# Routed experts of a decoder layer: rows beyond an expert's first 128 in float32 units of 32

## The chip, the cores and the metric

The kernel runs on one core of one Trainium2 chip, in one launch. The metric is the device time in microseconds. Its median over 3 runs is 2264.56 us (2258.63 to 2267.71) for the kernel before.

## The reference, cut to what matters

One layer of a decoder: a mixer with an output projection, then a mixture of experts, then a gated embedding. 2048 prompt rows and 8 sample rows of 1024 numbers go through it, all in float32. The change is in the experts:

```python
g_sel = argmax(softmax(x @ rg_w + rg_b))                 # one group of 4
top_v, top_i = top_k(e_logits[g_sel], 2)                 # two experts of its 8
expert_idx = g_sel * 8 + top_i                           # two of 32 experts for each row
y[rows of e] = (silu(x @ w1[e]) * (x @ w3[e])) @ w2[e]   # w1, w3: 1024 x 512, w2: 512 x 1024
h = h + weight_0 * y[first choice] + weight_1 * y[second choice]
```

So 4112 rows (two for each of 2056) are shared out over 32 experts. How many each gets follows from the inputs. The router of the reference, worked out on its inputs, gives for experts 0 to 31: 135, 135, 153, 129, 194, 186, 171, 89, 103, 161, 174, 73, 77, 88, 155, 115, 145, 78, 135, 127, 141, 177, 113, 138, 161, 102, 85, 101, 134, 120, 112, 105. 17 experts have more than 128 rows, most of them a few more.

## The kernel before

Phase one is the input projection and the recurrent part, phase two the output projection with norm and router (17 tiles of 128 rows), phase three the experts, and the last phase the gated embedding. In phase three each engine runs its own program, and semaphores tie them; no scheduler moves anything.

**Blocks.** An expert's rows are worked through in blocks of 128 (`block_of`), at least one for each expert. In all that is 49 blocks: 15 experts with one, 17 with two. `blk` holds the first and the end block of each expert, each engine reads them into registers (`span`), and a loop over registers runs the blocks. A weight is split into two float32r parts, `w_hi` (a rounded copy, on ScalarE, `copy` L2149) and `w_lo` (the remainder, on VectorE L2212, for one half of w1 on GpSimd L2070); so are the rows. A product is then three float32r matmuls, hi x hi, hi x lo and lo x hi. On TensorE a block is: 48 matmuls of 512 columns into H1 and H3 (L2113 to L2115), 8 transposes of the next block's rows (L2102) and 4 of `hid` (L2121), and 24 matmuls into the two banks Y (L2132, L2136).

**Weights.** Each of w1, w3, w2 of an expert is 2 MB and comes in two DMAs of 1 MB (`load`, on the SP queue) into one raw buffer for each of the three. A half is fetched again as soon as its split for the expert before is done (`reload`). Four slots of `w_hi` and `w_lo` turn round, so that splits run ahead of the blocks that need them (`parts_ahead`).

**Rows.** GpSimd fetches a list of 128 row numbers (`load_list`), then the rows by an indirect DMA (`gather`), one block ahead. ScalarE copies the result to `y_sb` and sends it to `y_dram`, one block late (`y_out`).

**Start and end of phase three.** Rows of `y_dram` behind the last block are filled at the start of phase three by up to 16 DMAs of 512 KB (L2034). `choices_rows`, on VectorE, works out from which rows of `y_dram` the last phase gathers; it stands behind the last block. The gate weights of the last phase (`in_w_ple_gate`) go through the raw buffers and the same splits as a 33rd expert.

## Time and profile before

| what | value |
|---|---|
| median of 3 runs | 2264.56 us |
| the profiled execution | 2255.27 us, span of its instructions 2253.7 us |
| first matmul of the first block to last matmul of the last | 1061.35 to 1965.96 us |
| TensorE busy over the span | 2149.3 us (95%) |
| VectorE, ScalarE, GpSimd busy | 1430.6 us (63%), 971.0 us (43%), 581.7 us (26%) |
| mean granted TensorE clock | 0.977 of 2.4 GHz |
| moved by DMA | 407.13 MB, 181 GB/s over the span |

Busy time of TensorE counts overlapping matmuls once, from the start of one to its modelled end. What a stream of matmuls costs is the distance from one start to the next. A float32r matmul leaves one pair of records (load of the stationary side, matmul); a plain float32 matmul leaves two such pairs.

### The profile page before, as it was taken

What the parts mean: (1) busy time and instruction counts of PE and PEld (TensorE: products, weight loads), DVE (VectorE), ACT (ScalarE), POOL (GpSimd) and SP (SyncE); (2) the same over time, 40 slices, a digit from 0 to 9 for tenths busy, and PEclk for the clock granted to TensorE, in tenths of its full rate; (3) what the DMA queues carried; (4) which work ended last, traced back from release to release, by engine and by line L of the source; (5) the groups of instructions that cost most, each with busy time, mean ns of one, the idle gap of its engine ahead of it and who ended that gap; (6) DMA issues with size and microseconds to landing.
All of it is one profiled execution on the core that took longest, in us unless ns stands there. A gap on an engine that the chain in (4) does not pass through costs nothing. (4 is left out here: it accounts for less than half of the span.)

```text
span 2253.7 us, 34056 instructions
## 1 busy us (share of the span) xinstructions
PE 2149.3 (95%) x10539; PEld 1773.2 (79%) x10540; DVE 1430.6 (63%) x2866; ACT 971.0 (43%) x1569; POOL 581.7 (26%) x595
## 2 busy tenths in 40 slices
PE   6999999999899999994889999999999999899998
PEld 5878888888788888884778888888888878767775
DVE  5788888888566665564536465665566566846554
ACT  4433344444432222222435465665556465623332
POOL 1121111111244333332121223233332132233332
PEclk9999999999999999996999999999999999999999
DMA  6111110132534333324787677898787778943441
GB/s 231 60 38 66 65 60 37 65 112 92 187 107 136 121 121 117 103 91 147 292 309 256 219 266 289 292 363 289 283 294 260 289 290 305 334 169 125 158 141 49
DMA packets 160333, 407.13 MB, mean 181 GB/s; under 512 B 18835, under 2 KB 22347, under 8 KB 160014
## 3 DMA queue, kind: packets, MB, share of 16 engines
q1 hardware_dynamic: 138518, 337.17, 42.0%
q0 software_dynamic: 14560, 43.11, 5.8%
q10 hardware_dynamic: 7200, 26.22, 2.9%
q8 instruction: 23, 0.38, 0.1%
q14 instruction: 32, 0.26, 0.0%
HBM read 330.12 MB, written 84.82 MB: 184 GB/s over the span
## 5 line engine op out<-in xcount | busy, mean ns | idle before, releaser
L234 PE MATMUL bank<-w_hi,mix_x 128*128 128x512 f32 x816 | 333.3, 408 | 9.9 <-DMA mix_x<-xT_dram 4.0
L236 PE MATMUL bank<-w_hi,mix_x 128*128 128x512 f32 x816 | 323.8, 397 | 0.0
L235 PE MATMUL bank<-w_lo,mix_x 128*128 128x512 f32 x816 | 322.9, 396 | 0.0
L2113 PE MATMUL bank<-w_hi,x_hi 128*128 128x512 f32 x784 | 307.6, 392 | 8.1 <-POOL w_lo L2070 4.6
L2212 DVE TENSOR_TENSOR w_lo<-raw,w_hi 128x2048 fp32r<-128x2048 f32 x130 | 292.6, 2311 | 34.8 <-ACT w_hi L2149 34.7
L2115 PE MATMUL bank<-w_hi,x_lo 128*128 128x512 f32 x784 | 307.1, 392 | 0.0
L2114 PE MATMUL bank<-w_lo,x_hi 128*128 128x512 f32 x784 | 307.1, 392 | 0.0
L2149 ACT ACTIVATE w_hi<-raw 128x2048 fp32r<-128x2048 f32 x130 | 238.8, 1925 | 4.8 <-DMA raw<-in_w 4.8
L2070 POOL TENSOR_TENSOR w_lo<-shared,w_hi 128x2048 fp32r<-128x2048 f32 x31 | 157.2, 5071 | 231.7 <-DMA shared<-hn_dram,entry 131.9
L234 PEld LDWEIGHTS bank<-w_hi,mix_x 128*128 128x128 f32 x816 | 156.7, 192 | 42.0 <-issue 5.1
L236 PEld LDWEIGHTS bank<-w_hi,mix_x 128*128 128x128 f32 x816 | 156.3, 192 | 34.7
L235 PEld LDWEIGHTS bank<-w_lo,mix_x 128*128 128x128 f32 x816 | 156.7, 192 | 29.9
L2113 PEld LDWEIGHTS bank<-w_hi,x_hi 128*128 128x128 f32 x784 | 148.5, 189 | 39.9 <-POOL w_lo L2070 5.0
L2115 PEld LDWEIGHTS bank<-w_hi,x_lo 128*128 128x128 f32 x784 | 148.4, 189 | 31.0
L2114 PEld LDWEIGHTS bank<-w_lo,x_hi 128*128 128x128 f32 x784 | 148.5, 189 | 30.9
L248 POOL TENSOR_SCALAR stat<-stat 128x4 f32<-128x4 f32 (+3 forms) x67 | 13.4, 200 | 514.2 <-ACT junk L716 271.2
L2061 POOL DMA_INDIRECT shared<-hn_dram,entry x49 | 68.2, 1392 | 282.9 <-DMA entry<-list_dram 139.3
L2149 ACT ACTIVATE hidT_hi<-bank 128x128 fp32r<-128x128 f32 x98 | 37.6, 384 | 226.3 <-PE bank L2121 226.3
L2217 DVE SCALAR_TENSOR_TENSOR up<-tanh_h,bank 128x512 f32<-128x512 f32 x49 | 33.5, 684 | 157.4 <-ACT tanh_h L2174 157.4
L2132 PE MATMUL bank<-w_hi,hidT_hi 128*128 128x512 f32 x392 | 126.6, 404 | 0.0
L2132 PE MATMUL bank<-w_lo,hidT_hi 128*128 128x512 f32 x392 | 122.3, 393 | 0.0
L2149 ACT ACTIVATE w_hi<-shared 128x2048 fp32r<-128x2048 f32 x64 | 119.7, 1921 | 4.7 <-DMA shared<-in_w 3.9
(316 smaller groups left out, 4222.1 us busy)
## 6 DMA issues: line engine op xcount, KB each, us to landing
raw<-in_w SPq DMA_DIRECT2D x128, 1024.0 KB, 8.5
shared<-in_w SPq DMA_DIRECT2D x64, 1024.0 KB, 8.6
y_dram<-y_sb ACTq DMA_DIRECT2D x50, 512.0 KB, 6.9
xT_dram<-mix_x SPq DMA_DIRECT2D x34, 512.0 KB, 3.5
mix_x<-xT_dram SPq DMA_DIRECT2D x34, 512.0 KB, 4.5
shared<-in_w_in SPq DMA_DIRECT2D x24, 512.0 KB, 6.5
small<-in_x_prompt SPq DMA_DIRECT2D x16, 512.0 KB
xr_sb<-in_x_prompt SPq DMA_DIRECT2D x16, 512.0 KB
```

The costliest lines, as they stand in the source:

```text
L234: pe.matmul(bank[:, :], x_hi[:, k, :], wh[:, k, :], start=(k == 0), stop=False)
L235: pe.matmul(bank[:, :], x_hi[:, k, :], wl[:, k, :], start=False, stop=False)
L236: ins = pe.matmul(bank[:, :], x_lo[:, k, :], wh[:, k, :], start=False, stop=(k == KD - 1))
L2061: pool.indirect_dma_start(out=rows_in[:, :], out_offset=None, in_=hn_dram[0:NT * P + NS, :], in_offset=bass.IndirectOffsetOnAxis(ap=entry[ ...
L2070: pool.tensor_tensor(w_lo[slot(j, 0)][:, cols], raw[0][:, cols], w_hi[slot(j, 0)][:, cols].bitcast(F32), ALU.subtract).then_inc(w1_lo, 1)
L2113: pe.matmul(bank[:, :], x_hi[:, k, :], wh[:, k, :], start=(k == 0), stop=False)
L2114: pe.matmul(bank[:, :], x_hi[:, k, :], wl[:, k, :], start=False, stop=False)
L2115: ins = pe.matmul(bank[:, :], x_lo[:, k, :], wh[:, k, :], start=False, stop=(k == KD - 1))
L2132: pe.matmul(Y[n][:, :], hidT_hi[:, k, :], col(w, k, n), start=(k == 0 and w is wh), stop=False)
L2149: return act.activation(out, in_, ACT.Copy)
L2212: dve.tensor_tensor(w_lo[slot(j, m)][:, cols], raw[m][:, cols], w_hi[slot(j, m)][:, cols].bitcast(F32), ALU.subtract).then_inc(w1_lo if is ...
L2217: STT(up[:, :], tanh_h[:, :], 1.0, H1[:, :], ALU.add, ALU.mult).then_inc(up_done, 1)
```

## The change

An expert's first 128 rows are computed as before, in one block of three float32r products (`expert` in place of the loop over `block_of`). Its rows beyond 128 are computed in units of 32 (`tail`), at least one for each expert, in plain float32 with the raw weights. With the counts above that makes 40 units: 25 hold rows, and 15 experts have one of unused rows; expert 4 has three, experts 5, 6, 9, 10, 21 and 24 have two.

A unit keeps its 32 rows (transposed, `xT_t`) as the stationary side and streams the weights. Four column tiles of the array each take a quarter of the hidden columns: of w1 and w3 together 256 columns, 8 times over the depth, so 32 matmuls; then 16 matmuls of 256 columns for w2. Units belong to one expert ahead: while expert e's block is computed, the units of expert e + 1 run, with raw w1, w3 (now in two buffers `raw13` that take turns) and w2; with the last block those of expert 0. In each round of the loop the 12 matmuls of `first_down` (one half of expert e's down projection, 512 columns each) stand between the unit's own steps. They start their bank anew in each round, so they are computed once for each unit.

The weights have three slots in place of four, and splits run at most one matrix ahead. The order on SP, GpSimd, ScalarE and VectorE is written anew around that. `choices_rows` now stands between two splits of the last expert. Unused rows of `y_dram` are filled in phase two, by one DMA of 258 rows from HBM to HBM in each of 16 tiles. The bounds of an expert's units are read into registers within the expert (on TensorE between the two lots of transposes). VectorE has 6 more small instructions of 32 columns where it works out `blk`.

```diff
+TAIL = 32
+TILES = P // TAIL
+MAXT = NE + (SEQ + NS) * 2 // TAIL
+SPARE = (MAXT + 1 - NE) * TAIL // NT
...
+                                if r == P:
+                                    sp_.dma_start(y_dram[bass.ds(u * SPARE + NE * (P + TAIL), SPARE), :], x_rows[0:SPARE, :]).then_inc(spare_filled, 16)
...
+                def behind(e):
+                    return 0 if isinstance(e, int) and e == NE - 1 else e + 1
...
+                        def expert(e, two, j):
+                            wait_lo(sp_, e, 2, 1)
+                            load(behind(e), 1 - j, 2)
+                            sp_.wait_ge(h3_mm, e + 1)
+                            for m in range(2):
+                                if last(e):
+                                    load_gate(m)
+                                else:
+                                    load(e + 2 if not isinstance(e, int) or e < NE - 2 else 0, j, m)
...
+                        def first_down(k):
+                            wh, wl = w_down(w_hi), w_down(w_lo)
+                            pe.matmul(Y[0][:, :], hidT_hi[:, k, :], wh[:, k, 0:512], start=(k == 0), stop=False)
+                            pe.matmul(Y[0][:, :], hidT_hi[:, k, :], wl[:, k, 0:512], start=False, stop=False)
+                            pe.matmul(Y[0][:, :], hidT_lo[:, k, :], wh[:, k, 0:512], start=False, stop=(k == KF - 1))
+
+                        def tail(i, e, two, j):
+                            for m in range(2):
+                                for c in range(2):
+                                    pe.wait_ge(*tail_in(e, two, j, m, c))
+                            pe.wait_ge(t_x_in, i + 1)
+                            w13 = raw13[1 - j][:, :].rearrange("p (m k n) -> p m k n", m=2, k=KD)
+                            for k in range(KD):
+                                for q in range(TILES):
+                                    ins = pe.matmul(UP_T[q * TAIL:(q + 1) * TAIL, :].rearrange("p (m n) -> p m n", m=2), xT_t[:, k, :],
+                                                    w13[:, :, k, q * P:(q + 1) * P], start=(k == 0), stop=(k == KD - 1))
+                            ins.then_inc(t_up_mm, 1)
...
+                            pe.wait_ge(hidT_lo_ready, 2 * e + 2)
+                            first_down(0)
+                            pe.wait_ge(t_rows, 16 * i + 32)
+                            first_down(1)
+                            tail_transposes()
+                            pe.wait_ge(t_hid, i + 1)
+                            pe.transpose(HID_T, hid_t[:, :], ident[:, :]).then_inc(t_hid_tp, 1)
+                            first_down(2)
+                            first_down(3)
...
+                            for k in range(KF):
+                                for q in range(TILES):
+                                    ins = pe.matmul(DOWN_T[q * TAIL:(q + 1) * TAIL, :], hidT_t[:, k * TAIL:(k + 1) * TAIL],
+                                                    w2[:, k, q * width:(q + 1) * width], start=(k == 0), stop=(k == KF - 1))
+                            ins.then_inc(t_down_mm, 1)
...
+                        def tail(i, e):
+                            act.wait_ge(t_up_mm, i + 1)
+                            act.activation(tanh_t[:, :], UP_T[:, 0:P], ACT.Tanh, scale=0.5).then_inc(t_tanh, 1)
+                            tail_x(i + 1)
+                            act.wait_ge(t_hid_tp, i + 1)
+                            copy(hidT_t[:, :], HID_T).then_inc(t_hidT_in, 1)
...
+                        def expert(e, two, j):
+                            split(e, two, j, 1)
+                            if not isinstance(e, int) or e > 0:
+                                y_halves(e - 1)
+                            split(e, two, j, 2)
+                            if not isinstance(e, int) or e > 0:
+                                y_out(e - 1)
+                            first, end = span(act, behind(e))
+                            act.wait_ge(h1_mm, e + 1)
+                            act.activation(tanh_h[:, :], H1[:, :], ACT.Tanh, scale=0.5).then_inc(tanh_done, 1)
+                            split(e + 1, *follow(two, j), 0)
```

TensorE, one block before, from the last up matmul to the end of the block (`bank` is a PSUM bank, `shared` here the gathered rows; in all fences of this part, register rows and rows that only repeat are left out):

```order
L2115 MATMUL bank<-w_hi,x_lo 128x512
L2102 MATMUL bank<-ident,shared 128x128 x4
L2121 MATMUL bank<-ident,hid 128x128
L2102 MATMUL bank<-ident,shared 128x128 x4
L2121 MATMUL bank<-ident,hid 128x128 x3
L2132 MATMUL bank<-w_hi,hidT_hi 128x512 x2
L2132 MATMUL bank<-w_lo,hidT_hi 128x512 x2
L2136 MATMUL bank<-w_hi,hidT_lo 128x512 x8
L1964 COMPARE_AND_BRANCH
```

And now, with the unit in its loop between the transposes and the second half of the down projection (`raw_1` holds raw w1 and w3 of the next expert; a row 32x256 is one column tile's matmul):

```order
L2222 MATMUL bank<-w_hi,x_pair 128x512
L2236 MATMUL bank<-ident,hid 128x128 x3
L2185 MATMUL bank<-raw_1,xT_t 32x256 x32
L2173 MATMUL bank<-w_hi,hidT_hi 128x512
L2167 MATMUL bank<-ident,rows_t 128x32 x8
L2198 MATMUL bank<-ident,up 128x128
L2175 MATMUL bank<-w_hi,hidT_lo 128x512
L2209 MATMUL bank<-shared,hidT_t 32x256 x16
L2238 COMPARE_AND_BRANCH
L2242 MATMUL bank<-w_hi,hidT_hi 128x512
```

48 matmuls of the new shape, 8 transposes of 32 rows and one of 128 came in; of the 24 down matmuls 12 stand inside the loop.

ScalarE, the last block before (both splits of the gate's first half stood ahead of it, the row L2149 on `shared`):

```order
L2149 ACTIVATE w_hi<-shared 128x2048 x2
L2174 ACTIVATE tanh_h<-bank 128x512
L2149 ACTIVATE y_sb<-bank 128x512 x2
L2149 ACTIVATE hidT_hi<-bank 128x128
L2149 ACTIVATE hidT_hi<-bank 128x384
L2149 ACTIVATE x_hi<-bank 128x512 x2
L2149 ACTIVATE w_hi<-raw 128x2048 x2
```

ScalarE, the last expert now (`raw_1` in the first of these rows on it holds the gate's first half):

```order
L2312 ACTIVATE tanh_h<-bank 128x512
L2256 ACTIVATE w_hi<-raw_1 128x2048 x2
L2256 ACTIVATE hidT_hi<-bank 128x128
L2256 ACTIVATE hidT_hi<-bank 128x384
L2276 ACTIVATE tanh_h<-bank 128x128
L2256 ACTIVATE xT_t<-bank 128x256
L2256 ACTIVATE hidT_t<-bank 128x128
L2256 ACTIVATE y_t<-bank 128x256
```

The split of the gate's first half moved from ahead of the last block's tanh to behind it, and stands ahead of the copies of `hidT_hi` there.

VectorE, the last expert now (`shared` in the rows of L2365 to L2371 is scratch room):

```order
L2351 TENSOR_TENSOR w_lo<-raw_1,w_hi 128x2048 x2
L2363 TENSOR_SCALAR rowbase<-lead 128x34
L2365 TENSOR_TENSOR shared<-rowbase,ecap 128x1088
L2371 TENSOR_REDUCE rowbase<-shared 128x34
L2351 TENSOR_TENSOR w_lo<-shared,w_hi 128x2048 x2
L2385 SCALAR_TENSOR_TENSOR up<-tanh_h,bank 128x512
L2394 TENSOR_TENSOR hidT_lo<-bank,hidT_hi 128x384
L2351 TENSOR_TENSOR w_lo<-raw_1,w_hi 128x2048 x2
L2356 SCALAR_TENSOR_TENSOR up<-tanh_h,bank 128x128
```

`choices_rows` (L2363 to L2373) stands ahead of the split of w2 and of `up`, and the split of the gate's first half ahead of the unit's own first step; before, both came outside the last block.

## Rows read from the trace of the kernel before

**Rows 1.** The page: busy time by engine, then the span in 40 slices
```profile
PE 2149.3 (95%) x10539; PEld 1773.2 (79%) x10540; DVE 1430.6 (63%) x2866; ACT 971.0 (43%) x1569; POOL 581.7 (26%) x595
...
PE   6999999999899999994889999999999999899998
...
PEclk9999999999999999996999999999999999999999
```

**Rows 2.** Windows (us, each engine's busy us, PEclk, DMA share, GB/s)
```profile
1153.00:1368.00 215.00, 214.53 (x1008) 176.82 (x1007) 117.93 (x119) 113.59 (x127) 54.65 (x31) 1.00 0.73 262
...
1060.00:1065.00 5.00, 3.65 (x9) 2.88 (x10) 3.28 (x3) 3.32 (x2) 0.00 (x0) 0.50 0.95 361
...
1075.00:1080.00 5.00, 4.53 (x27) 3.97 (x27) 2.83 (x6) 1.75 (x4) 0.58 (x1) 1.00 1.05 400
...
954.00:1008.00 54.00, 54.00 (x285) 45.80 (x283) 31.68 (x105) 14.77 (x40) 19.11 (x23) 1.00 0.25 84
```

**Rows 3.** Timeline of TensorE: blocks' first matmuls (start us, length us), last end
```profile
1061.35 0.79 PE L2113 MATMUL bank<-w_hi,x_hi 128*128 128x512 f32 x1 [3.53 <-DVE x_lo L2204]
...
1152.93 0.39 PE L2113 MATMUL bank<-w_hi,x_hi 128*128 128x512 f32 x1
...
1296.60 0.39 PE L2113 MATMUL bank<-w_hi,x_hi 128*128 128x512 f32 x1
...
1314.50 0.39 PE L2113 MATMUL bank<-w_hi,x_hi 128*128 128x512 f32 x1
...
1964.67 1.29 PE L2136 MATMUL bank<-w_hi,hidT_lo 128*128 128x512 f32 x5
```

**Rows 4.** Groups of the page: shapes xcount, busy us, mean ns, idle before
```profile
L2113 PE MATMUL bank<-w_hi,x_hi 128*128 128x512 f32 x784 | 307.6, 392 | 8.1 <-POOL w_lo L2070 4.6
L2212 DVE TENSOR_TENSOR w_lo<-raw,w_hi 128x2048 fp32r<-128x2048 f32 x130 | 292.6, 2311 | 34.8 <-ACT w_hi L2149 34.7
L2149 ACT ACTIVATE w_hi<-raw 128x2048 fp32r<-128x2048 f32 x130 | 238.8, 1925 | 4.8 <-DMA raw<-in_w 4.8
L2070 POOL TENSOR_TENSOR w_lo<-shared,w_hi 128x2048 fp32r<-128x2048 f32 x31 | 157.2, 5071 | 231.7 <-DMA shared<-hn_dram,entry 131.9
```

**Rows 5.** The chain that ended last: 24 float32r matmuls, 4 float32 (8 records)
```profile
2007.66 5.48 PE bank L2414 x24
2013.14 3.43 PE bank L2399 x8
```

**Rows 6.** Timeline of TensorE: eight transposes; matmuls with 8 output partitions
```profile
1982.51 1.04 PE L2390 MATMUL bank<-ident,hs 128*128 128x128 f32 x8
...
2222.86 0.66 PE L2390 MATMUL bank<-ident,hs 8*128 8x8 f32 x8
...
2228.96 0.39 PE L2414 MATMUL bank<-w_hi,hT_lo 128*128 128x512 f32 x1
2229.28 3.60 PE L2399 MATMUL bank<-shared,hz 128*8 128x512 f32 x8
2232.81 0.50 PE L2414 MATMUL bank<-w_hi,hT_hi 128*128 128x512 f32 x1
2233.14 0.40 PE L2414 MATMUL bank<-w_lo,hT_hi 128*128 128x512 f32 x1
```

**Rows 7.** DMA issues: KB each, median us to landing
```profile
raw<-in_w SPq DMA_DIRECT2D x128, 1024.0 KB, 8.5
...
entry<-list_dram POOLq DMA_DIRECT2D x50, 0.5 KB, 4.7
shared<-hn_dram,entry POOLq DMA_INDIRECT x50, 6.4
```

**Rows 8.** Timelines of the last block: ScalarE, VectorE
```profile
1965.46 1.13 ACT L2149 ACTIVATE y_sb<-bank 128x512 f32<-128x512 f32 x2
...
1962.73 0.17 DVE L2233 TENSOR_SCALAR rowbase<-lead 128x34 f32<-128x34 f32 x1
...
1967.14 4.49 DVE L2212 TENSOR_TENSOR w_lo<-raw,w_hi 128x2048 fp32r<-128x2048 f32 x2
```

**Rows 9.** Timeline of SP in phase two: the load of rows, once in each tile
```profile
850.70 0.33 SPq L1203 DMA_DIRECT2D xr_sb<-in_x_prompt  x1
...
877.47 0.33 SPq L1203 DMA_DIRECT2D xr_sb<-in_x_prompt  x1
```

More of the change, by code:

```diff
@@ L2187, in _ @@
-                        act.sem_inc(y_stored, 16)
+                            if not last(e):
+                                x_halves(e + 1)
+                            with act.Fori(first, end) as i:
+                                tail(i, e)
+                        act.sem_inc(t_stored, 16)
+                        act.sem_inc(t_y_in, 1)
                         x_halves(0)
-                        split(0, 0, 1)
-                        split(0, 0, 2)
-                        all_blocks(act, block_of, after)
+                        each_expert(act, expert)
@@ L2242, in choices_rows @@
                             dve.wait_ge(place_steps, 4)
[L2243 removed]
+                            STT(yrow[:, :, :], rowbase[:, :, :], float(-NE * (CAP - P) - P), place[:, :, :], ALU.add, ALU.add).then_inc(place_steps, 1)
                             dve.wait_ge(place_steps, 5)
[L2246 to L2251 removed]
```

474 lines of the change are left out of this document (270 added, 204 removed).

## The prediction

> **What bounds the kernel now.** I read the page first: TensorE is busy 95% of the span, next VectorE with 63%, and TensorE's busy share is 8 or 9 tenths in nearly every slice [rows 1]. The windows say the same of phase three: of 215 us TensorE is busy 214.53, VectorE 117.93, ScalarE 113.59, at the full clock, with DMA at 0.73 [rows 2]. So a change in phase three is worth what it takes from TensorE's stream plus what it adds in waits. The timeline gives the price of a block: one begins at 1296.60, the next at 1314.50, 17.90 us [rows 3]. The count is 784 / 16 = 49 blocks [rows 4], which the row counts of the 32 experts give too. 49 x 17.90 = 877.1 us of the 904.6 between 1061.35 and 1965.96; the other 27.5 are stalls. The first four blocks take 91.6 us instead of 71.6, 20.0 lost while the weights of three experts come in; the remaining 45 take 813.0 instead of 805.5, 7.5 lost [rows 3].
>
> The prices on TensorE: 24 float32r matmuls of 512 columns in 5.48 us are 0.228 each [rows 5]. Four float32 matmuls of 512 columns (8 records) take 3.43 us [rows 5], so one of 256 columns takes 0.43 us by itself. Eight 128 x 128 transposes start 0.109 us apart (1.04 less the last one's length, over 7), eight of 8 x 8 about 0.065 apart [rows 6]; I take the latter as what one pair of weight load and short matmul costs at the least.
>
> **The change part by part, for TensorE.** The sum is made against the profiled execution, 2255.27 us, 0.4% under the median of 2264.56; I add its result to the median.
>
> Removed: 17 second blocks, 17 x 17.90 = -304.3 us. What is left of a block stays as it was: 48 + 12 + 12 matmuls and 12 transposes.
>
> Added: 40 units. Each has 32 + 16 = 48 float32 matmuls of 256 columns. The trace has no neighbouring matmuls in different column tiles, so their overlap is the unknown price. Bounds: all four tiles at once, 48 x 0.43 / 4 = 5.2 us; none at once, 48 x 0.43 = 20.6 us. With full overlap the 96 pairs also cost 96 x 0.065 = 6.2 us if the pairs are what limits. For the likeliest case I take full overlap, and 5.6 us, between 5.2 and 6.2, since part of the pairs can be issued ahead while longer matmuls run.
> Nine transposes: 8 of 32 rows between 0.065 and 0.109 each, one at 0.109: 0.8 us.
> Changes between wide and narrow outputs: from 2228.96 to 2229.28 lie 0.32 us where 0.23 is the pitch, so going in costs 0.09; coming out, 8 records of 0.429 end at 2232.71, the next matmul starts at 2232.81 and its follower 0.33 later instead of 0.23, 0.2 in all [rows 6]. Twice in and out per unit: 0.6 us.
> Sum of a unit 7.0 us, x 40 = +280. In 8 of the units the 12 matmuls of `first_down` are computed once more: 8 x 12 x 0.228 = +21.8.
> Stream in all: -304.3 + 280 + 21.8 = -2.5 us. The work saved and the work added are nearly equal, because 15 experts pay for a unit of unused rows.
>
> Steps within a unit that could make TensorE wait: from the end of the up matmuls, tanh on ScalarE and two steps on VectorE of 128 columns, some 1.2 us, lie beside two lots of `first_down` (1.4) and the transposes (0.8); the two copies to `hidT_t` and `xT_t` beside the other two lots (1.4). I cost these at nothing; without that cover they cost about 1 us each, +40 to +80 us in all.
>
> **Other engines.** With one unit an expert takes 17.9 + 7.0 = 24.9 us. ScalarE then has six splits of 1.9 [rows 4] and some 5 us of copies, 17 us; VectorE five of 2.3 and some 4.5, 16 us; GpSimd one of 5.1 and the issue of two gathers, whose list and rows land 4.7 and 6.4 us after it [rows 7], a unit or an expert ahead. All under 24.9. The tightest place is w3: ScalarE splits it after the unit's last copy, 2 x 1.9 us, then VectorE 2.3 more, some 7.0 us with the copy; TensorE wants it after 12 down matmuls and 24 up, 8.2 us. It fits with 1.2 us to spare. Cost zero.
>
> DMA: an expert brings 6.3 MB of weights, 0.5 of rows, 0.5 of results, some 0.3 for the unit. At the 400 GB/s that a full DMA share shows [rows 2] that is 19 us of 24.9. w2 of the next expert is asked for about 1.2 us before the end of h3, and wanted by the unit's down matmuls 8 to 9 us after it; 2 MB at 400 GB/s are 5.3 us, plus the 2 to 3 us that a DMA of 1 MB with nothing ahead needs besides (8.5 us to landing, median, mostly for two in flight [rows 7]). It just fits.
>
> Fill of unused rows: 1.06 MB per tile in phase two, where TensorE has no idle time and the DMA share is 0.25 [rows 2]. At 400 GB/s that is 3 to 5 us of DMA per tile of 26.8 us (850.70 to 877.47 [rows 9]), well before the loads of the next mixer rows. Cost 0, at the most 16 x 1 us. In turn the start of phase three is rid of 8 MB.
>
> **Start of phase three.** The first unit needs w1 and w3 of expert 1; w3 and w2 of expert 0 stand ahead of them: 8.4 MB from 1057 on at 400 GB/s, landed at about 1079 to 1081. TensorE would be there at about 1077, after a first block that runs in part at half the clock (PEclk 0.50 up to 1065 [rows 2]). So 4 us of wait and 3 of clock, less what later experts wait: 6 us where 20 were lost, -14. The 7.5 us of later stalls also go, since the weights have 24.9 us for each expert: -7.
>
> **Last expert.** Here two things are new. `choices_rows` takes 4.4 us (1962.73 to 1967.14 [rows 8]) and stands ahead of the split of w2. And ScalarE must split the gate's first half before it copies `hidT_hi`, but SP asks for the gate weights after the end of h3 and behind w2 of expert 0: about 4 MB after that, 13 to 15 us to landing of the second half, then the split of 1.9. TensorE meanwhile has only the unit's up matmuls. `hidT` comes about 18 us after h3 instead of 2, then VectorE splits two halves (4.5 us) before the unit's own steps. The expert ends 31 us after h3 instead of 14: +17. Results are copied behind one more split (3.7 us) where they were copied at once (1965.46 [rows 8]): +3, since the last gathers wait for them.
>
> Sum: -2.5 - 14 - 7 + 17 + 3 = -3.5 us, so 2264.56 - 3.5 = 2261 us. Within full overlap the ends are 6.4 us for a unit (-24 us, -27 in all) and 7.8 (6.2 + 1.0 + 0.6; +32, +28 in all, together with 0.5 us here and there for the loop's branches): 2236 to 2292.
>
> **Rivals.**
> *Overlap of two, not four (36%).* A float32 matmul leaves two pairs of records one behind the other [rows 5]. If TensorE starts matmuls strictly in order and the second pass must wait until the first has left its tile, then only the second pass of one tile and the first of the next run together. A matmul then costs one pass, 0.214 us, up to 0.24 with the start: 48 x 0.214 = 10.3, to 11.5 us. That is +4.7 to +5.9 us a unit, +188 to +236 in all, some 5 less for waits that it hides: 2445 to 2490 us. This is the rival on the other side; it decides as soon as a unit's 48 matmuls take more than about 5.9 us (+0.5%). For it speaks the order in the trace; against it, that nothing in the trace shows a busy tile holding up another.
> The Trainium skill ("TensorE: Matmul & The Clock Gate", Part 3, What overlaps and what doesn't) says that matmuls keep strict program order in start and end, which is the premise of this rival; its Measured speedup section gives 2.38 for three column tiles, one matmul in each, which is the premise of full overlap. By the one the kernel takes some 2465 us, by the other about 2261; no run of before shows either.
> *The units are cheap (27%).* The pairs are no limit and the transposes take 0.065: 6.4 us a unit, 2238 us, 2230 to 2252. For it: TensorE's queue can run ahead while 0.228 us matmuls are in front.
> *No overlap at all (5%).* 48 x 0.43 = 20.6 us: +15 x 40 = +600, 2860 us. Only if float32 excludes tiles side by side.
> *The last expert or the start costs more than I see (in the 32% of the likeliest).* A clock that falls in the wait would add up to 5 us.
>
> **Chances.** Full overlap 59%: of it 27% cheap units (faster), 32% around my number, of which some 3 faster, 20 within 0.5% (2253 to 2276; about what a measurement of this kernel can tell from no change), 9 slower. Overlap of two 36%, none 5%. So faster 0.30, same 0.20, slower 0.50. The likeliest case is full overlap, with its own range 2236 to 2292; since a third of the chance lies at 2445 to 2490, the range for 8 in 10 goes from 2236 to 2490, leaving out the case of no overlap and the thin ends.
>
> **What would show it.** In the changed kernel's timeline: 40 rounds of 48 matmuls in narrow tiles; the 32 of the up part span 3.5 to 4.2 us with full overlap, 6.9 to 7.7 with two, 13.7 with none. Experts with one unit begin 24.9 us apart (29.6 to 30.8; 39.9). The first expert is some 6 us longer, in the last one TensorE idles about 10 us before `first_down`, released by ScalarE's `hidT_hi`, which waited for `in_w_ple_gate`. Idle time of TensorE at w3's `w_lo` or at raw w2 in most experts would show my two margins (1.2 us, and the DMA of w2) wrong. Phase two should keep its 27 us a tile.

## The result and the profile after

The changed kernel takes 2297.53 us (median of 4 runs, 2296.34 to 2298.68) beside 2261.6 for the kernel before on the same chip: ratio 1.0156, 95% interval 1.0129 to 1.0183, slower by 36 us. The profiled execution took 2297.97 us, its span is 2296.4 against 2253.7. The spans differ by 42.7 us where the medians differ by 36, because the profiled execution of before (2255.27 us) is faster than any of the four behind its median; what follows accounts for the 42.7.

The page of after, lines that answer to [rows 1] and [rows 7]: busy time, TensorE by slices, the granted clock, then DMA issues (KB each, median us to landing), the third of them the new fill of unused rows.

```profile
span 2296.4 us, 39441 instructions
PE 2159.8 (94%) x13407; PEld 1680.9 (73%) x13408; DVE 1445.2 (63%) x2830; ACT 966.7 (42%) x1607; POOL 651.5 (28%) x641
PE   6999999999999999994899999999999999789998
PEclk9999999999999999996999999999999999899999
raw<-in_w SPq DMA_DIRECT2D x130, 1024.0 KB, 15.7
mix_x<-xT_dram SPq DMA_DIRECT2D x34, 512.0 KB, 5.3
y_dram<-in_x_prompt SPq DMA_DIRECT2D x16, 1032.0 KB, 8.0
```

The windows of phase three, first after, then before (busy us and count of each engine, clock, DMA share, GB/s; the other end of each window is the end of the last block):

```profile
1085.00:2007.00 922.00, 885.85 (x6984) 631.29 (x6984) 546.17 (x469) 502.70 (x574) 320.25 (x173) 0.98 0.74 273
```

```profile
1061.00:1966.00 905.00, 885.64 (x4116) 728.45 (x4116) 533.28 (x509) 510.08 (x539) 251.29 (x128) 0.99 0.80 291
```

TensorE's busy time in phase three is the same to 0.2 us: 17 blocks went, and 40 units with 8 repeated `first_down` weigh as much. What grew is idle time, 19 to 36 us. The other part of the loss lies ahead of phase three. By the timeline, the first block starts at 1085.16 where it started at 1061.35 [rows 3]. The difference of the spans is therefore 42.7 us = 23.8 before the first block + 17.5 in phase three (922.1 us for 904.6) + 1.4 behind it.

### The profile page after: what moved, and what is told of

It reads as the page before. It is cut to its first block and busy times, and to the rows that moved or that the text cites. A ratio compares the mean times of both kernels' runs of the same rounds, so it can differ in the third digit from the quotient of the medians.

```text
span 2296.4 us, 39441 instructions
## 1 busy us (share of the span) xinstructions
PE 2159.8 (94%) x13407; PEld 1680.9 (73%) x13408; DVE 1445.2 (63%) x2830; ACT 966.7 (42%) x1607; POOL 651.5 (28%) x641
## 5 line engine op out<-in xcount | busy, mean ns | idle before, releaser
L2220 PE MATMUL bank<-w_hi,x_pair 128*128 128x512 f32 x512 | 203.8, 398 | 12.8 <-DVE w_lo L2351 8.7
L2222 PE MATMUL bank<-w_hi,x_pair 128*128 128x512 f32 x512 | 200.6, 392 | 0.0
L2221 PE MATMUL bank<-w_lo,x_pair 128*128 128x512 f32 x512 | 200.6, 392 | 0.0
L2121 POOL TENSOR_TENSOR w_lo<-raw,w_hi 128x2048 fp32r<-128x2048 f32 x31 | 141.8, 4575 | 197.6 <-ACT w_hi L2256 197.5
L2351 DVE TENSOR_TENSOR w_lo<-shared,w_hi 128x2048 fp32r<-128x2048 f32 x66 | 148.4, 2288 | 16.7 <-PEq L1204 10.9
L2185 PE MATMUL bank<-raw,xT_t 128*32 128x256 f32 x2560 | 150.9, 389 | 2.2 <-DMA raw<-in_w 2.2
L2113 POOL DMA_INDIRECT rows_t<-hn_dram,entry_t x40 | 63.8, 1595 | 291.2 <-DMA entry_t<-list_dram 198.3
L2220 PEld LDWEIGHTS bank<-w_hi,x_pair 128*128 128x128 f32 x512 | 96.7, 189 | 44.8 <-DVE w_lo L2351 20.9
L2185 PEld LDWEIGHTS bank<-raw,xT_t 128*32 128x32 f32 x2560 | 81.4, 112 | 60.5 <-issue 12.8
L2559 PE MATMUL bank<-w_hi,hT_hi 128*128 128x512 f32 x272 | 113.9, 419 | 2.0 <-DVE hT_lo L2632 2.0
L871 DVE SCALAR_TENSOR_TENSOR qkT<-qkin,cwt,qkT 128x128 f32<-128x128 f32 x384 | 110.3, 349 | 3.4
L2222 PEld LDWEIGHTS bank<-w_hi,x_pair 128*128 128x128 f32 x512 | 96.7, 189 | 20.7
```

What stands on the lines that cost most here:

```text
L871: st.do(STT(cv[:, k, :], src, cwt[:, k, j:j + 1], cv[:, k, :], ALU.mult, ALU.add))
L2121: pool.tensor_tensor(w_lo[0][:, cols], raw_of(e, j, 0)[:, cols], w_hi[0][:, cols].bitcast(F32), ALU.subtract).then_inc(w1_lo, 1)
L2185: ins = pe.matmul(UP_T[q * TAIL:(q + 1) * TAIL, :].rearrange("p (m n) -> p m n", m=2), xT_t[:, k, :], w13[:, :, k, q * P:(q + 1) * P], sta ...
L2220: pe.matmul(bank[:, :], x_hi[:, k, :], wh[:, k, :], start=(k == 0), stop=False)
L2221: pe.matmul(bank[:, :], x_hi[:, k, :], wl[:, k, :], start=False, stop=False)
L2222: ins = pe.matmul(bank[:, :], x_lo[:, k, :], wh[:, k, :], start=False, stop=(k == KD - 1))
```

## Where the time lies in the trace

**The unit.** TensorE's timeline of after, an expert with one unit:

```profile
1496.68 0.49 PE L2236 MATMUL bank<-ident,hid 128*128 128x128 f32 x3
1497.10 3.66 PE L2185 MATMUL bank<-raw,xT_t 128*32 128x256 f32 x64
1500.69 0.50 PE L2173 MATMUL bank<-w_hi,hidT_hi 128*128 128x512 f32 x1
...
1502.28 0.68 PE L2167 MATMUL bank<-ident,rows_t 32*128 32x32 f32 x8
1503.26 0.33 PE L2198 MATMUL bank<-ident,up 128*128 128x128 f32 x1 [0.30 <-DVE up L2358]
...
1504.91 1.93 PE L2209 MATMUL bank<-shared,hidT_t 128*32 128x256 f32 x32
1506.78 0.50 PE L2242 MATMUL bank<-w_hi,hidT_hi 128*128 128x512 f32 x1
```

Read starts, not lengths: the up part holds TensorE for 1500.69 - 1497.10 = 3.59 us (64 records, two for each float32 matmul), the down part for 1506.78 - 1504.91 = 1.87. Together 5.46 us for 48 matmuls, 0.114 each where I took 0.43 for one by itself. The starts of the single records, which the timeline puts together into one row, show how: in all 40 units they come in fours, the four within some 0.02 us and the next four 0.216 us later at the full clock. Each matmul has two records, so a step of four matmuls takes 2 x 0.216 = 0.43 us, the price that I took for one: the four column tiles overlap in full.

**Phase two.** SP's timeline of after (issue of the load of rows, then the fill, then a sample's state; answers to [rows 9]):

```profile
841.34 0.33 SPq L1209 DMA_DIRECT2D xr_sb<-in_x_prompt  x1
841.71 0.52 SPq L1238 DMA_DIRECT2D y_dram<-in_x_prompt  x1
842.89 0.43 SPq L1276 DMA_DIRECT2D shared<-in_state_C  x1
870.21 0.33 SPq L1209 DMA_DIRECT2D xr_sb<-in_x_prompt  x1
...
901.97 0.33 SPq L1209 DMA_DIRECT2D xr_sb<-in_x_prompt  x1
```

These two tiles take 28.9 and 31.8 us where one took 26.8 [rows 9]; from 902 on, where no state is loaded any more, it is 26.6 again. The fill stands ahead of the state's load on the same queue. The six loads of the state land 7.5 to 13.0 us after their issue where they took 4.8 to 5.6. What VectorE waits for, 600 to 1040 us (us in total, times, longest), before and after:

```profile
DVE shared L1679 <- DMA shared<-in_state_C: 3.6, 6, 0.9
```

```profile
DVE shared L1687 <- DMA shared<-in_state_C: 33.4, 6, 9.0
```

**First and last expert.** TensorE's timeline of after, rows that waited (in brackets us, releaser): the first expert, then the last.

```profile
1105.56 0.47 PE L2236 MATMUL bank<-ident,hid 128*128 128x128 f32 x1 [5.33 <-ACT xT_t L2256]
1109.70 6.11 PE L2185 MATMUL bank<-raw,xT_t 128*32 128x256 f32 x64 [2.17 <-DMA raw<-in_w]
...
1979.34 1.37 PE L2236 MATMUL bank<-ident,hid 128*128 128x128 f32 x4 [3.93 <-DVE hid L2390]
1980.64 5.84 PE L2185 MATMUL bank<-raw,xT_t 128*32 128x256 f32 x64
1994.63 0.77 PE L2173 MATMUL bank<-w_hi,hidT_hi 128*128 128x512 f32 x1 [8.15 <-DVE hidT_lo L2394]
```

The up part, 3.66 us long elsewhere, takes 5.8 to 6.1 behind such waits. Windows of after on the up part of the first expert, of the one shown above, and of the last (columns as for the windows above):

```profile
1109.80:1115.30 5.50, 5.50 (x60) 2.67 (x64) 2.28 (x1) 0.00 (x0) 3.55 (x3) 0.55 1.03 395
1497.20:1500.60 3.40, 3.40 (x64) 1.88 (x64) 2.87 (x2) 1.47 (x3) 3.33 (x1) 1.00 1.03 418
1980.70:1986.00 5.30, 5.30 (x61) 2.59 (x64) 0.00 (x0) 0.00 (x0) 0.00 (x0) 0.58 1.03 415
```

The granted clock was 0.55 and 0.58 of 2.4 GHz behind the idle time, near the lower of its two levels, and 1.00 where TensorE had been busy. The DMA share is full in all three windows, so it does not tell them apart. The up part of the first expert starts 24.5 us behind the first block, when the raw weights of expert 1 have landed. SP's timeline shows one reason why they are late:

```profile
1079.45 0.96 SPq L2058 DMA_DIRECT2D raw<-in_w  x2
1083.99 0.88 SPq L2058 DMA_DIRECT2D shared<-in_w  x2
1084.91 6.61 SPq L2058 DMA_DIRECT2D raw<-in_w  x3
```

The first row is w3 of expert 0. SP then waits for two splits (`lo_ready`, `w1_lo`) before it asks for w2 and for the weights of expert 1, 4.5 us later, at 1083.99. In the last expert, ScalarE and VectorE show what TensorE's 8.15 us wait for:

```profile
1988.73 1.91 ACT L2256 ACTIVATE w_hi<-raw 128x2048 fp32r<-128x2048 f32 x1 [16.85 <-DMA raw<-in_w_ple_gate]
1993.55 0.94 DVE L2394 TENSOR_TENSOR hidT_lo<-bank,hidT_hi 128x128 fp32r<-128x128 f32 x2 [13.80 <-ACT hidT_hi L2256]
```

ScalarE waits 16.85 us for the gate's weights, and its copy of `hidT_hi` stands behind their split. The first expert takes 39.2 us, the last 43.3. In between, 23 experts with one unit take 25.63 us on average (25.65 where the unit is empty, 25.62 where it holds rows), and a further unit 8.81.

## The experiments

| kernel | median us | ratio to before (95%) | first block | phase three | behind it |
|---|---|---|---|---|---|
| before | 2261.6 | | 1061.4 | 904.6 | 287.7 |
| after | 2297.5 | 1.0156 (1.0129 to 1.0183) | 1085.2 | 922.1 | 289.2 |
| b_fill | 2281.0 | 1.0095 (1.0074 to 1.0116) | 1084.1 | 907.4 | 287.8 |
| a_fill_later | 2276.7 | 1.0076 (1.0059 to 1.0092) | 1065.2 | 920.5 | 289.0 |
| a_fill_act | 2284.4 | 1.0103 (1.0085 to 1.0121) | 1073.7 | 921.9 | 289.2 |
| a_last | 2283.9 | 1.0102 (1.0085 to 1.0119) | 1084.9 | 904.5 | 293.8 |
| a_down_by_tile | 2405.6 | 1.0635 (1.0610 to 1.0661) | 1094.5 | 1025.4 | 288.8 |
| a_two_units | 2509.7 | 1.1104 (1.1077 to 1.1132) | 1081.8 | 1131.6 | 288.9 |
| a_early_gate | 2266.0 | 1.0015 (1.0003 to 1.0026) | 1067.2 | 910.0 | 288.9 |
| a_skip | 2240.0 | 0.9902 (0.9884 to 0.9921) | 1067.2 | 885.6 | 292.9 |
| a_skip_all | 2216.3 | 0.9792 (0.9776 to 0.9808) | 1067.7 | 858.0 | 288.8 |
| a_first_x | 2217.6 | 0.9803 (0.9790 to 0.9817) | 1066.3 | 860.8 | 290.2 |

The last three columns are the start of the first block, from there to the end of the last, and the rest of the span, in us of the profiled execution. Each ratio is taken to the kernel before as measured beside that run, 2260.7 to 2262.1 us. Four kernels have the phase two of after (after, a_last, a_down_by_tile, a_two_units), and their first blocks start between 1081.8 and 1094.5: a start of one execution holds to some us, and so does the 23.8.

**b_fill: the fill alone, in the kernel before.**

```diff
+        fill_dram = dram("fill_dram", (NT * SPARE, D))
...
+                                if r == P:
+                                    sp_.dma_start(fill_dram[bass.ds(u * SPARE, SPARE), :], x_rows[0:SPARE, :]).then_inc(place_filled, 16)
```

> The kernel before, with one addition: the 16 DMAs of 258 rows from HBM to HBM in phase two, at the same place on the SP queue as in the changed kernel, into a tensor that nothing reads. Phase three is untouched, its own fill too. In the changed kernel the first block starts at 1085.2 us instead of 1061.4. Theory A (the fill alone did that): the first block starts 20 to 24 us later, the kernel takes 20 to 26 us more than before, about 2283 to 2288. Theory B (the delay comes from something else in the change to phase two, such as other semaphores, the buffers' places in memory or the 6 more small steps on VectorE): within 5 us of before.

Measured: +20 us, the first block 22.7 us later. The same wait as in after:

```profile
DVE shared L1684 <- DMA shared<-in_state_C: 30.8, 6, 6.4
```

So the fill by itself costs what phase two lost, and nothing of the new expert code is needed for it (SP waits for the 16 fills ahead of phase three here; the last one has landed 37 us before SP issues the first load there, so this wait costs nothing).

**a_fill_later: the same 16 fills, behind the loads of the state on SP's queue.**

```diff
                                 if past(u, 0):
                                     keep_hn(u - 1, r_last)
+                                    sp_.dma_start(y_dram[bass.ds((u - 1) * SPARE + NE * (P + TAIL), SPARE), :], x_rows[0:SPARE, :]).then_inc(spare_filled, 16)
...
-                                if r == P:
-                                    sp_.dma_start(y_dram[bass.ds(u * SPARE + NE * (P + TAIL), SPARE), :], x_rows[0:SPARE, :]).then_inc(spare_filled, 16)
```

> The changed kernel with the fill of a tile moved on the SP queue: behind the loads and stores of the sample states of its tile and the store of its normalised rows, ahead of the next tile's mixer loads. Theory A1 (order on the queue: what is issued right behind the fill, the sample states of 256 KB above all, lands later and VectorE waits for it): 15 to 24 us less than the changed kernel, 2274 to 2283, and VectorE's wait for in_state_C falls from 33 us to about 4. Theory A2 (bandwidth: 17 MB more to move delay whatever runs beside them): within 6 us of the changed kernel, 2292 to 2300, with the wait moved to other loads.

Measured: 20.8 us of the 36 come back, and the wait is as before:

```profile
DVE shared L1686 <- DMA shared<-in_state_C: 4.3, 6, 0.9
```

The bytes are the same, so it is the place that cost: the fill ran in front of a load that was wanted at once. Not all of it comes back: in the five kernels with this order the first block starts 3.8 to 6.3 us later than in before. What this rest waits for stays open.

**a_fill_act: the fill at the old moment, but from ScalarE's queue.**

```diff
-                                if r == P:
-                                    sp_.dma_start(y_dram[bass.ds(u * SPARE + NE * (P + TAIL), SPARE), :], x_rows[0:SPARE, :]).then_inc(spare_filled, 16)
...
                                 act.wait_ge(h_ready, u + 1)
+                                if r == P:
+                                    act.dma_start(y_dram[bass.ds(u * SPARE + NE * (P + TAIL), SPARE), :], x_rows[0:SPARE, :]).then_inc(spare_filled, 16)
```

> The changed kernel with the same fill issued at the same moment (when the rows of h are ready) from ScalarE's queue instead of SP's. Theory A1 (order on SP's queue): 15 to 24 us less than the changed kernel, 2274 to 2283. Theory A2 (bandwidth beside the state loads): within 6 us of the changed kernel, the wait of VectorE for in_state_C stays above 25 us.

Measured: 13.1 us come back, not 21. The wait and the landing of the state (256 KB; 5.3 us before, 8.5 in after, 5.4 in a_fill_later):

```profile
DVE shared L1687 <- DMA shared<-in_state_C: 18.3, 6, 4.0
```

```profile
shared<-in_state_C SPq DMA_DIRECT2D x6, 256.0 KB, 8.4
```

The median is as in after, but the six landings lie between 7.9 and 9.4 us and none takes 13.0, and the longest wait is 4.0 us instead of 9.0. Another queue helps only in part: running at the same time costs some 8 us of the 21, standing behind the fill on one queue some 13. The Trainium skill ("DMA: Bandwidth & Descriptors", Issuing engines are not separate DMA queues) says that queues of different issuing engines run on the same 16 DMA engines; the 8.4 us here agree.

**a_last: the last expert's order mended.** ScalarE copies the results first and splits both halves of the gate behind the units, VectorE does the same with its half of these splits, and `choices_rows` stands behind `hidT_lo` (ScalarE's lines are shown).

```diff
-                            split(e + 1, *follow(two, j), 0)
+                            if not last(e):
+                                split(e + 1, *follow(two, j), 0)
...
                         each_expert(act, expert)
-                        split(NE, NE // 2, 0, 1)
                         y_halves(NE - 1)
                         y_out(NE - 1)
+                        split(NE, NE // 2, 0, 0)
+                        split(NE, NE // 2, 0, 1)
```

> The changed kernel with the last expert mended: ScalarE and VectorE split the gate's first half behind the last unit instead of ahead of hidT and of the unit's steps, the results of the last expert are copied and sent ahead of these splits, and choices_rows stands behind hidT_lo. In the changed kernel the last expert takes 43.3 us and TensorE idles 4.3 us ahead of hid's transposes and 8.5 us ahead of first_down. If these waits are what I took them for: last expert 26 to 28 us, both waits gone, and 13 to 18 us less in all, 2280 to 2285. If TensorE waits there for the DMA of the unit's raw w2 anyway, the last expert stays above 35 us. The splits behind the last unit could delay the last phase instead: then the gap from the last down matmul to the first gate matmul grows by as much as the expert gets shorter.

Measured: phase three is 17.6 us shorter, 904.5, but the first product of the gate starts 26.1 us behind the last block where it was 21.5, so 13.6 us are kept. The last expert takes 25.9 us, as much as any other, so its price was order; part of it belongs to the gate's split, which has to be done somewhere. The edits were made together, so the share of each is not known.

**a_down_by_tile: the 16 down matmuls of a unit tile by tile.**

```diff
-                            for k in range(KF):
-                                for q in range(TILES):
+                            for q in range(TILES):
+                                for k in range(KF):
```

> The kernel after, with the down part's 32 matmuls of a unit written tile by tile (eight steps of the sum of one column tile, then the next tile) where they stood step by step with the four tiles side by side. Same work, same result. Theory A (four column tiles run at the same time because matmuls that stand next to each other go to different tiles): matmuls of one tile behind one another cannot overlap, so the down part goes from 1.9 us to near four times that, 6.8 us or more, and the kernel gets 40 x 5.0 = 200 us longer, about 2490. Theory B (a narrow float32 matmul of 256 columns is this cheap by itself, whatever stands beside it): the down part stays at 1.9 us and the time within 10 us of 2297.

Measured: +108 us to after, 2.7 us for each of 40 units. Its timeline, the up part (unchanged) and the down part, with the next start:

```profile
1499.09 3.66 PE L2185 MATMUL bank<-raw,xT_t 128*32 128x256 f32 x64
...
1506.91 4.59 PE L2209 MATMUL bank<-shared,hidT_t 128*32 128x256 f32 x32
1511.43 0.50 PE L2242 MATMUL bank<-w_hi,hidT_hi 128*128 128x512 f32 x1
```

(The expectation says eight steps of one tile's sum; it is four matmuls, eight records.) The down part holds TensorE 4.52 us instead of 1.87. So the overlap does come from neighbours in different tiles (theory B falls). It is not the 6.8 us of theory A, which took it that nothing overlaps in this order. The starts of the 32 records are the same in all 40 units: four alone, 0.216 to 0.24 us apart, then twelve times two within 0.03 us, then four alone, again 0.216 apart. So a matmul that runs alone costs two times 0.216 = 0.43 us, as I had scaled it, and the 0.28 us that come out on average are a mean of lone records and pairs. The pairs say one thing more. The first tile has eight records, but from the fifth on they come by twos. As the first four show, records of one tile do not run side by side, so the second tile's must have started beside the first tile's last four, ahead of their place in the program. This is worked out from the starts; the trace does not name a record's tile.

**a_two_units: at least two units for each expert, 65 in all.**

```diff
-                            TS(rt[:, 0, :], blk[:, 1, :], 1.0, None, ALU.max)
+                            TS(rt[:, 0, :], blk[:, 1, :], 2.0, None, ALU.max)
```

> The kernel after, with at least two units for an expert where one was the least: the 25 experts that had one unit get an empty second one, so 65 units run where 40 did. Nothing is left out. It prices a unit with the part of the first expert half that is done over with it. Theory A (the price of a further unit is the 8.75 us that the experts with two units show against those with one): +25 x 8.75 = +219 us, 2516. Theory B (experts with one unit already pay waits that a second unit does not add to, and the two-unit experts of the trace are special because they wait for memory): 25 x 6.5 = +160 us, about 2460.

Measured: +212 us for 25 more units, 8.5 each: the unit 5.8, its `first_down` 2.7. Theory A holds. The experts with a full and an empty unit take 34.05 us here, those with two full ones 34.38 in after: an empty unit costs as much as a full one.

**a_early_gate: a_fill_later, and the last expert with the gate's weights asked for early.** SP asks for them once this expert's up weights are split; VectorE and ScalarE leave `choices_rows` and the second half's split until the units are done, the results go out first.

```diff
+                            if last(e):
+                                sp_.wait_ge(tails_done, NE - 1)
+                                for m in range(2):
+                                    for c in range(2):
+                                        wait_lo(sp_, e, m, c)
+                                    load_gate(m)
+                                wait_lo(sp_, e, 2, 1)
+                                load(behind(e), 1 - j, 2)
+                                return
```

> The kernel after with the two things mended that the earlier runs priced: the fill stands behind the reads of the next tile on SP's queue (alone 2276.7), and in the last expert the gate's weights are asked for as soon as the up weights are split, the rows of choices and the split of the gate's second half follow the units, and ScalarE gives its half of the results out ahead of that split. Theory A (the last expert's two waits of 4.3 and 8.5 us are order on DVE and can be hidden in full, since the gate then starts with its weights there): 2276.7 - 17 = 2260, within 5 us of the kernel before. Theory B (as in the run with the split put last, what leaves the last expert comes back at the gate): 2270 to 2277.

Measured: 2266.0, between the figures of the two theories and just inside the 5 us of theory A (4.5 above before). The last expert takes 30.5 us instead of 43.3, and nothing comes back at the gate (288.9 behind it). Its waits in TensorE's timeline (answers to the last rows of after above):

```profile
1958.60 1.01 PE L2244 MATMUL bank<-ident,hid 128*128 128x128 f32 x4 [0.45 <-DVE hid L2395]
1959.55 3.66 PE L2193 MATMUL bank<-raw,xT_t 128*32 128x256 f32 x64
1965.91 0.33 PE L2206 MATMUL bank<-ident,up 128*128 128x128 f32 x1 [0.41 <-DVE up L2366]
1970.63 3.55 PE L2217 MATMUL bank<-shared,hidT_t 128*32 128x256 f32 x32 [3.00 <-issue]
```

The 8.15 are gone; 3.0 us are new at the down part, and it runs 3.5 us instead of 1.87 behind them. By my reading they wait for w2 of expert 0, now behind the gate's weights on SP's queue: its two halves are issued from 1956.87 to 1957.8, with 12.2 us to landing (median), which is about 1970. The kernel is within 0.2% of before. In the profiled executions its first block still starts 5.8 us later and phase three is 5.4 longer.

**a_skip: the up and down matmuls of an empty unit left out.** On a_early_gate, with a third row of `blk` that is 1 where an expert has rows beyond 128; TensorE branches on it. The results of empty units, which nobody reads, are left uncomputed.

```diff
+                            TS(blk[:, 2, :], blk[:, 1, :], 0.0, 1.0, ALU.max, ALU.min).then_inc(rank_steps, 1)
...
+                            with pe.If(used):
...
+                                for k in range(KD):
+                                    for q in range(TILES):
+                                        ins = pe.matmul(UP_T[q * TAIL:(q + 1) * TAIL, :].rearrange("p (m n) -> p m n", m=2), xT_t[:, k, :],
+                                                        w13[:, :, k, q * P:(q + 1) * P], start=(k == 0), stop=(k == KD - 1))
+                                ins.then_inc(t_up_mm, 1)
+                            with pe.Else():
+                                pe.wait_ge(t_x_in, i + 1)
+                                pe.sem_inc(t_up_mm, 1)
```

> The last kernel with the up and down matmuls of an empty unit left out by a branch on TensorE (15 of the 40 units hold no row; their results go to rows that nobody reads, so nothing that counts is left out). Theory A (the units' matmuls are paid in full on TensorE, 5.45 us and two changes of mode a unit): 15 x 5.5 to 6 us less, -82 to -90 against the kernel without the branch, near 2175, faster than the kernel before by 3 to 4%. Theory B (what the matmuls leave, the chain of tanh, product and transpose on the other engines takes up, since the transpose of the unit's hidden rows waits for it): 2 to 3 us a unit, -30 to -45, near 2220. Theory C (the branch costs an instruction load of some us on every unit, 40 of them): no gain or a loss, 2255 to 2300.

Measured: 26 us less than a_early_gate, 1.7 for each of the 15 empty units: the mechanism of theory B, with less left over than its 2 to 3 us. What TensorE waits for, 1100 to 1900 us:

```profile
PE bank L2211 <- DVE up L2379: 31.6, 15, 2.6
PE bank L2182 <- DVE hidT_lo L2412: 17.7, 14, 1.3
PE bank L2240 <- DVE w_lo L2372: 4.2, 9, 0.6
```

15 times 2.1 us at the transpose of the hidden rows (L2211): the steps on VectorE that the up matmuls used to cover. Its timeline in one such expert shows which:

```profile
1447.46 3.25 DVE L2372 TENSOR_TENSOR w_lo<-raw,w_hi 128x2048 fp32r<-128x2048 f32 x1
1450.63 0.27 DVE L2377 SCALAR_TENSOR_TENSOR up<-tanh_h,bank 128x128 f32<-128x128 f32 x1
1450.93 0.29 DVE L2379 SCALAR_TENSOR_TENSOR up<-up,bank 128x128 f32<-128x128 f32 x1
```

The unit's own two steps are short; what holds them is the next expert's split, which stands ahead of them on VectorE. The first row is one instruction and takes 3.25 us where such a split takes 2.29 by itself: GpSimd's own split runs beside it for the first 1.1 us. 14 waits of 1.3 us for `hidT_lo` are new as well. The clock takes part too: from 1100 to 1900 us the granted clock is 0.97 here, where it is 1.00 in a_early_gate and in a_skip_all, so some of what the next run gives back is clock.

**a_skip_all: that transpose left out too.**

```diff
+                            with pe.If(used):
+                                pe.wait_ge(t_hid, i + 1)
+                                pe.transpose(HID_T, hid_t[:, :], ident[:, :]).then_inc(t_hid_tp, 1)
+                            with pe.Else():
+                                pe.wait_ge(t_xtp, i + 2)
+                                pe.sem_inc(t_hid_tp, 1)
```

> As the last kernel, with the transpose of an empty unit's hidden rows left out too, so that TensorE doesn't wait for the chain of tanh and products of an empty unit before the down part's place; it waits for it there, 2.3 us later. Nothing that counts is left out. Theory A (in the last run the empty units gave 1.7 us each and not 5.5 because TensorE waited for VectorE's products ahead of that transpose, 34.4 us in all from 1100 to 1950 us, and ran at half clock behind the waits): those waits go and 2.3 to 3.5 us a unit come back, 2240 - 15 x 2.3 to 3.5 = 2190 to 2205. Theory B (the experts with an empty unit are by now bound by something beside TensorE, the splits on VectorE and ScalarE or the loads of 3 MB of weights, which at the 290 GB/s of that stretch are 10.8 us and cannot be it): the wait only moves to the next expert's first block, and the time stays at 2235 to 2242.

Measured: 2216.3, 24 us less again, 1.6 a unit, below the 2.3 of theory A; faster than before by 2.1% (1.9 to 2.2) and than after by 81 us. The same view:

```profile
PE bank L2182 <- DVE hidT_lo L2417: 19.0, 15, 1.3
PE bank L2268 <- DVE up L2384: 17.1, 15, 1.2
PE bank L2245 <- DVE w_lo L2377: 4.9, 13, 0.6
```

Of the 2.1 us, 1.1 came back ahead of the second half of the down projection (L2268): in the down part's place the branch for an empty unit waits for `hid_t`, the same product on VectorE behind the same split. That split stands there in all runs; moving it behind the unit's steps was not tried. An expert with an empty unit takes 21.8 to 22.8 us instead of 25.65; one with a single full unit 25.3 to 25.8 (25.5 to 26.0 in after). Expert by expert that is between 0.3 less and 0.2 more, so what the branches cost is at most 0.2 us.

**a_first_x: ScalarE's copy of the first unit's rows ahead of the split that stood in front of it.**

```diff
+                            if isinstance(e, int) and e == 0:
+                                tail_x(0)
                             split(e + 1, *follow(two, j), 0)
-                            if isinstance(e, int) and e == 0:
-                                tail_x(0)
```

> The last kernel (2216) with two lines of ScalarE exchanged in the first expert: the copy of the first unit's transposed rows stands ahead of the split of the second expert's up weights, where it stood behind it. Nothing is left out. In the kernel after, the first expert took 39.2 us where I had forecast 31; TensorE waits there 4.6 to 5.3 us for this copy, which waits on ScalarE behind a split that waits for a load, and 2.2 us more for the load itself, and the unit's up part runs at half clock behind these waits (5.8 us). Theory A (what is late is the load of the weights of the expert ahead, which this unit needs in its raw form; the copy only names it first): the wait moves to the up part, the first expert keeps 38 to 39 us and the time 2214 to 2218. Theory B (the order on ScalarE is what delays it): 4 to 5 us less, 2211, and the first expert 34.

Measured: 2217.6, no gain; the first expert takes 38.8 us (38.3 in a_skip_all). The rows that waited:

```profile
1082.03 0.30 PE L2262 MATMUL bank<-ident,hid 128*128 128x128 f32 x1 [0.35 <-DVE hid L2413]
1091.30 5.37 PE L2195 MATMUL bank<-raw,xT_t 128*32 128x256 f32 x64 [8.21 <-DMA raw<-in_w]
```

The wait for the copy is gone and stands whole, 8.21 us, at the load of raw w1 and w3 of expert 1: theory A. What binds the first expert is that its unit needs the next expert's weights, which land 25 us behind the first block's start in this kernel too.

## Why the prediction was right and wrong

The likeliest number was 2261, the time is 2297.5: inside the range that I gave for 8 in 10, but outside the likeliest case's own range of 2236 to 2292. That it is inside at all is luck: the range reached over the gap between full overlap (to 2292) and overlap of two (from 2445), and no case had its number there. I forecast 3.5 us less, which a measurement cannot tell from no change, and it came 36 us more. Of the four cases, full overlap came true. "Slower" had 0.50, but 0.41 of that stood for the two rivals of less overlap, and the loss has other causes.

- **Overlap, the disputed price: right.** 5.46 us for 48 matmuls where I took 5.6, and a_down_by_tile shows that interleaving the tiles makes it. The records set no limit of their own, as I had feared with my 96 x 0.065: four start within 0.02 us, and 24 steps of 0.216 are 5.2, my lower bound. The premise of the rival, that starts keep the order of the program, does not hold either: a matmul's two records stand next to each other in the program, but a four can hold at most one of each tile. The stream, -2.5 us in my sum, came out at +0.2 us of TensorE's busy time.
- **"Fill of unused rows ... Cost 0, at the most 16 x 1 us": the step that failed.** It cost 23.8 us up to the first block, more than even the 16 that I allowed and left out of the sum. I divided its bytes by the rate and looked at the next mixer loads, and did not ask what is issued right behind it on SP: the load of a sample's state, which VectorE was already waiting for (its longest wait 0.9 us before, 9.0 in after). b_fill and a_fill_later show this from both sides. DMA share 0.25 says nothing of a load with no slack.
- **First expert, wrong by 8.2 us.** I expected 31 us and "6 us where 20 were lost"; it took 39.2. I had the right cause, the first unit's weights, but put their landing 18 to 20 us behind the first block's start, where they landed 24.5 behind it: SP waits for two splits before it asks for them, and windows of after between 1084 and 1110 us show 315 to 390 GB/s where I took 400. a_first_x shows that the load sets it. The up part at half clock behind the wait added 2.2 us more; my 3 us of clock were those of the block's start.
- **Experts with one unit, 24.9 us, in truth 25.63.** The unit's steps against my 5.6 + 0.8 + 0.6: matmuls 5.46, transposes with a wait of 0.3 for `up` 1.07, and 0.37 for w3's `w_lo`, the margin of 1.2 us that I had called enough; some 0.8 is left for changes of shape and the loop. The wait for `up` comes from VectorE, to which I gave five splits of 2.3 us: in 22 experts one of them takes 4.4 to 4.5, since GpSimd's split runs beside it. Over the experts from the second to the last but one this makes +22 us, and further units at 8.81 instead of 7.0 + 2.7 give 7 back.
- **Last expert: right.** 43.3 us for 41.9, with 12 us of idle time (3.9 ahead of the transposes of `hid`, 8.15 ahead of `first_down`); the second ends as forecast with `hidT_hi`, behind the gate's DMA. a_last takes both away, a_early_gate most of it. What follows it lost 1.4 us for my 3.

Sum of the misses: 23.8 + 8.2 + 14.7 + 1.4 - 1.6 = 46.5 us; with my -3.5 that is +43.0, against the 42.7 of the spans. Half of it is one line of SP's program in the wrong place. Two small things: my sum says 21.8 for 96 x 0.228, which is 21.9, and what a change between wide and narrow outputs costs was not measured by itself.

The count of units explains why the change had so little to win from the start. 15 of 40 units hold no row and cost 7.7 us each (25.63 less the 17.9 of a block). With the fill and the last expert mended the kernel is level with before (a_early_gate); a_skip_all, which skips the empty units on TensorE, is what makes the change pay.

## What to carry to other kernels

Before a transfer is called free, look at the instruction that is issued next on its queue and at who waits for it, not at the queue's share of time: here 1 MB that nobody waits for cost 1.5 us a tile on average, and at most 0.4 once it stood behind the loads that were wanted. When work is cut into smaller units, price the empty ones as full ones and ask whether a branch can leave them out; then look at what the skipped work had covered on the other engines; here it was a split that stood ahead of two short steps. A wait that the trace puts down to a copy can be a load: move the copy, and see whether the wait moves on.

## What the runs showed of the hardware

- Float32 matmuls with 32 output partitions, 128 deep, 256 columns: 0.114 us each when the program takes the four column tiles in turn, 0.28 on average when one tile's stand next to each other (a_down_by_tile). The records start four at a time in the one order, one or two at a time in the other, and the next 0.216 us later; one alone costs 0.43. The Trainium skill ("TensorEngine Tiling (Array Packing)", Key Properties) says that different tiles can load weights and multiply in parallel; these numbers agree.
- A transfer from HBM to HBM of 1 MB lands in 8.0 us (median). A 256 KB load behind it on the same queue lands in 8.5 instead of 5.3 us, at worst in 13.0; with the transfer on another queue it is 8.4, at worst 9.4.
- VectorE's and GpSimd's float32 subtractions do not both run at full speed side by side. VectorE's split of 128 x 2048 takes 2.29 us, and in phase three it is longer only where GpSimd's split runs beside it, by nearly the time that they share: in after this meets 23 of 153 between 1090 and 1950 us, which take 3.5 to 4.5 us. In before one took longer (5.2 us), while 8 of GpSimd's 31 splits took 6.4 instead of 4.6 us.
- Three branches on TensorE in the loop of one unit cost at most 0.2 us together where the unit holds rows; an expert whose empty unit they skip takes 3.4 us less (a_skip_all).
